# A three-pass matmul kernel of seven layers: another order of products and weight splits at the seams between phases

## Chip, cores, metric

One Trainium2 chip, one core. The metric is device time in microseconds of one execution, from the first instruction to the last with what lies around them. Engines: PE (matmul and transposes), DVE (vector), ACT (scalar), POOL (GpSimd), SP (issues the weight loads).

## What is computed

Sequence 256, width 1024, all in float32. The first block is a short-convolution mixer and a SwiGLU network, then sliding-window attention and a second SwiGLU. The second block is a SwiGLU, a latent-attention and retention layer, a last SwiGLU and a final norm. Each sublayer reads a normalised copy of the running state `h` and adds its branch to it:

```
h = h + rmsnorm(short_conv_mixer(rmsnorm(h, g0)), p0)        # MIX,  8 column blocks
h = h + rmsnorm(swiglu(rmsnorm(h, g1)), p1)                  # FFN1, 11 blocks
h = h + rmsnorm(attention(rmsnorm(h, gkv), rmsnorm(h, gq)), p2)
h = h + rmsnorm(swiglu(rmsnorm(h, g3)), p3)                  # FFN2
h = h + 0.5 * swiglu_2(rms_norm(h, g4))                      # FFN3
h = h + concat(mla(n), retention(n)) @ w_o, n = rms_norm(h, g5)
h = h + 0.5 * swiglu_2(rms_norm(h, g6))                      # FFN4
out = rms_norm(h, final_norm)
```

## The kernel before

The 256 rows are two row tiles, t = 0 and t = 1, of 128 rows. Every float32 product is made in three passes (L1626): high part of x times high part of w, high times low, low times high. So every weight chunk (128 x 1024) is split once: ACT copies it to a rounded high part (`w_high`, L1026), DVE subtracts to get the low part (`w_low`, L1295). Split chunks lie in a ring of 12 slots; chunk c + 12 can be split only when row tile 1 has used chunk c. SP loads raw chunks four ahead into a ring of four (L821 to L828), a load starting when the split of the chunk four before it is done.

Making x for a phase takes this chain for each row tile: `turn` (eight PE transposes of `h` into pG and pT, L1656; DVE multiplies them by the gain into `hg`, L1321; ACT squares `h`, L1052), then `parts` (ACT rounds to `xTh`, L1058; DVE subtracts to `xTl`, L1328; POOL makes the norm factor). The attention needs a second x from the same transposes with another gain: `second` (L1071, L1341), which makes `x2h` and `x2l`.

A phase of blocks (MIX, FFN1 to FFN4) goes block by block: G (the products into pG, 24 matmuls of 512 columns for an FFN, of 384 for MIX), an activation on ACT and DVE (L1114, L1414), T (two transposes, then `aTh` on ACT, L1134, and `aTl` on DVE, L1433; in MIX a convolution with `aTh` and `aTl` made by step Y), D (the product back into pD: 12 matmuls, in MIX 6). At the end of a branch, `tail` squares it on ACT (L1101), POOL makes its norm factor, DVE multiplies by the post gain (L1392), and `join` adds it to `h` on DVE (L1404, two halves). FFN3, the latent layer and FFN4 have no post norm, so their `join` alone follows the product.

One written-out list of steps is walked by every engine (`walk`, L517): each engine issues its own part of each step, in the order of the list, and its queue is strictly in that order. So the place of a step in the list sets both when PE reaches it and what stands in front of it on ACT and DVE. Step R and the helper `refill` (L149) issue splits: ACT's `w_high` and DVE's `w_low` of as many chunks as are named, from the list `freed` of used slots.

The seams are hand-written. `walk_last_follower` (L232) is the end of a phase: G of row tile 1's last block, the `turn` of row tile 0 for the next phase behind it, D of the block before, `parts` of row tile 0, T, and splits. Row tile 1's last product and tail (`end_of`, L536, which calls `last_product`, L249) are left to the next phase: in FFN phases they run behind the first G (`open_end`, L166), followed by T, `refill` of all that is freed, and `join` of row tile 1. Attention and latent phases have no such hook: the last product and join come before them (L545, L550).

The attention's projections are `project(j, t, c)`: column group j (0 reads x, 1 and 2 read x2), row tile t, weight chunk c; four chunks make one group of 24 matmuls (5.5 us). With c == 3 ACT empties the group's bank to `qkv` (L1151). Before a product of row tile t starts, PE waits for that tile's x parts:

```
high, low = (x2h, x2l) if j else (xTh, xTl)
if c % 2 == 0:
    pe.wait_ge(xT_ready[t], xT_base(B_INDEX) + (2 if j else 0) + c // 2 + 1)
```

Then `rope` (L1441, rotary on DVE for the first part), QKT (transposes of q and k; DVE copies `qT`, L1458), S (scores), E, N, PT, PV. In the latent phase `project(i, t, c)` is the like for five groups (group 0 has 416 columns and is emptied to `lat`, L1193), and LAT(t) is three transposes of `lat`. `finish` (L1077 on ACT, L1347 on DVE, L995 on POOL) is the final norm and the stores.

Of the kernel before, what the change touches and what calls it, by code (L numbers as in the profile page):

```python
# [31 lines left out]
ALU = mybir.AluOpType  # L32
# [175 lines left out]
def walk_follower(ph, b, shift, step, freed):  # L208

    if ph.mixer and b == 1:  # L210
        walk_second_follower(ph, shift, step, freed)
        return
    g, first, last = ph.g_chunk(b), b == 0, b == ph.nb - 1
    early = (0 if ph.mixer else 2) if first else 1 if ph.mixer else 3
    step("R", g, early, shift)
    step("G", 1, b, shift)
    if not ph.mixer:
        step("R", g + early, ph.cg - early, shift)
        early = ph.cg
    if not first:  # L220
        step("D", 1, b - 1, shift)
    if ph.mixer:
        step("R", g + early, ph.cg - early, shift)
    if not first:
        step("T", 1, b, shift)
    if not first and not last:
        step("R", ph.d_chunk(b - 1), ph.kd, shift)
    if ph.mixer and not first:
        step("Y", 1, b, shift)


def walk_last_follower(ph, step, freed):  # L232

    b = ph.nb - 1
    g = ph.g_chunk(b)
    early = 0 if ph.mixer else 3
    step("R", g, early, 0)
    step("G", 1, b, 0)
    step("turn", 0, ph.index + 1)
    step("D", 1, b - 1, 0)  # L240
    step("parts", 0, ph.index + 1)
    step("T", 1, b, 0)
    if ph.mixer:
# [12 lines left out]
def walk_phase(eng, ph, step, trips, freed, open_end=None):  # L256

    per = RING // (ph.cg + ph.kd)
    start = 3 if trips else ph.nb
    for s in range(start):  # L260
        walk_block_step(ph, s, 0, step, freed, open_end)
    if trips:
        with eng.Fori(0, trips) as turn:
            for s in range(start, start + per):
                walk_block_step(ph, s, turn, step, freed)
        for s in range(start + per * trips, ph.nb):
            walk_block_step(ph, s, 0, step, freed)
# [10 lines left out]
    step("join", 0, ph.index)  # L278
    walk_last_follower(ph, step, freed)


def walk_attention(step, freed):


    def project(j, t, c):
# [4 lines left out]
    def projects(j, t, cs=range(4)):  # L290
        for c in cs:
            project(j, t, c)
# [4 lines left out]
            freed.append(B_WO + kt)  # L297

    projects(0, 0, range(3))
    walk_prep(step, 1, B_INDEX)  # L300
    project(0, 0, 3)
    step("second", 0)
    refill(step, freed)
    projects(0, 1)
    step("second", 1)
    refill(step, freed, 2)
    projects(1, 0)
    step("rope", 0, 0)
    refill(step, freed)
    step("exp_table",)  # L310
# [78 lines left out]
    output(1, 3)  # L389
    step("join", 0, B_INDEX)  # L390
    output(1, 4)
    refill(step, freed, 4)
    walk_prep(step, 0, B_INDEX + 1)
    for kt in range(5, 7):
        output(1, kt)
    refill(step, freed, 2)


def walk_latent(step, freed):


    def project(i, t, c):
# [13 lines left out]
            freed.append(C_WO + kt)  # L416

    projects(0, 0)
    walk_prep(step, 1, C_INDEX)
    refill(step, freed, 2)  # L420
    projects(1, 0)
    step("LAT", 0)
    refill(step, freed)
    projects(0, 1)
# [92 lines left out]
def walk(eng, step):  # L517
    freed = []
    step("start",)
    step("turn", 0, 0)  # L520
    step("first", 0, 0, FIRST_BEFORE_TURN)
    step("parts", 0, 0)
    step("turn", 1, 0)
    step("first", 0, FIRST_BEFORE_TURN, KT)
    step("fill", 0, 1)
    step("G", 0, 0, 0, ph=MIX)
    step("first", 1, 0, KT // 2)
    step("fill", 1, 1)
# [16 lines left out]
    end_of(FFN1)  # L545
    step("join", 1, FFN1.index)
    walk_attention(lambda *a: step(*a, ph=None), freed)
    walk_phase(eng, FFN2, lambda *a: step(*a, ph=FFN2), 4, freed, end_of_attention)
    walk_phase(eng, FFN3, lambda *a: step(*a, ph=FFN3), 4, freed, lambda: end_of(FFN2))
    end_of(FFN3)  # L550
    step("join", 1, FFN3.index)
    walk_latent(lambda *a: step(*a, ph=None), freed)
    walk_phase(eng, FFN4, lambda *a: step(*a, ph=FFN4), 3, freed)


# [10 lines left out]
def build(nc, x_in, stream, consts_in, table_in, pos_in, posts_in, out):  # L566
    with ExitStack() as ctx:
# [445 lines left out]
        def _(sc):  # L1013
# [61 lines left out]
                return sc.activation(hg[t][:, cols], hg[t][:, cols], ACT.Copy, scale=rr[t])  # L1075

            def finish(ph):  # L1077
                left, right, third, fourth = slice(0, 512), slice(512, 1024), slice(512, 768), slice(768, 1024)
# [6 lines left out]
                sc.wait_ge(h_ready[1], 2 * (LAST - 1) + 3)  # L1085
                sc.activation(junk[1][:, fourth], h[1][:, fourth], ACT.Square, scale=D ** -0.5,
                              accum_out=ss_end).then_inc(ss_ready[1], 1)
# [192 lines left out]
        def _(ve):  # L1280
# [66 lines left out]
            def finish(ph):  # L1347
# [23 lines left out]
                branch_done(ve, 1, k, 1)  # L1371
                ve.wait_ge(h_ready[1], 2 * k + 2)
                added(1, fourth, pT[0][:, 0:256])
                ve.wait_ge(ss_ready[1], 2 * LAST + 2)
                chain(ve.tensor_scalar(ms[1], ss[1][:, 0:1], ss[1][:, 1:2], EPS, ALU.add, ALU.add))
                joined()
                ve.wait_ge(ss_ready[1], 2 * LAST + 3)
                ve.tensor_scalar(ms[1], ms[1], ss_end, None, ALU.add).then_inc(end_m, 1)
                ve.wait_ge(h_ready[1], 2 * k + 3)
# [709 lines left out]
```

## Time and profile before

| what | value |
|---|---|
| median of 3 runs | 1074.96 us (1074.68 to 1077.29) |
| the profiled execution's own time | 1074.11 us |
| its span, first to last instruction | 1072.2 us |
| PE busy | 1055.5 us, 98% |
| PE weight loads | 872.1 us, 81% |
| DVE busy | 655.8 us, 61% |
| ACT busy | 560.9 us, 52% |
| POOL busy | 101.4 us, 9% |
| chain that ended last, PE's share | 89% |
| share of it of DVE's split of low parts | 3% |
| mean granted clock of TensorE | 0.999 |

The execution's own time is 1.9 us above its span, which lies around the span. The phases follow each other in the trace at about 105 us (FFN1's first product), 296 (attention), 376 (FFN2), 562 (FFN3), 753 (latent), 879 (FFN4) and 1060 (finish). A row of the time order gives start, length, engine, line, operation, what is written and read, count, and in brackets the idle time of the engine before it and who ended it; rows with a count above 1 are merged, and their length is from the first start to the last end. A PE row's length is modelled and overlaps the next one.

### The profile page before, as it was taken

To read this page: it belongs to the slowest core of one execution; us is meant where nothing else is said; L and a number is where in the kernel's file an instruction comes from. 1 tells how busy PE (TensorE), PEld (TensorE's weight loads), DVE (VectorE), ACT (ScalarE), POOL (GpSimd) and SP (SyncE) were. 2 spreads that over 40 slices of the span, in tenths; PEclk is the share of its full clock that TensorE was granted. 3 is DMA by queue.
4 is the path that set the end of the run, shared out by engine and by line. 5 is a ranking of instruction groups with operands and counts; after the bars stand their busy time and mean duration, and the time that the engine had idled before them with its cause. 6 is when DMAs were issued, how large, how long until landed. Compare 5 with 4: busy or idle time off the path is not lost.

```text
span 1072.2 us, 14824 instructions
## 1 busy us (share of the span) xinstructions
PE 1055.5 (98%) x5047; PEld 872.1 (81%) x5047; DVE 655.8 (61%) x930; ACT 560.9 (52%) x907; POOL 101.4 (9%) x194
## 2 busy tenths in 40 slices
PE   9999999999999999999999999999999999999997
PEld 6898888888787788888888888887888888888886
DVE  5867654545787864554666455466568674645543
ACT  5756544544667664444555444455476534444542
POOL 0034000000012041000001000000027120000001
PEclk9999999999999999999999999999999999999999
DMA  8664546556561454645565465556545133646541
GB/s 337 197 232 157 181 160 210 181 171 215 196 196 61 136 180 159 223 165 196 192 205 174 157 225 158 202 194 215 159 157 177 61 122 114 202 165 220 162 152 40
DMA packets 51884, 187.81 MB, mean 175 GB/s; under 512 B 5808, under 2 KB 5952, under 8 KB 51840
## 3 DMA queue, kind: packets, MB, share of 16 engines
q1 hardware_dynamic: 50688, 183.79, 51.3%
q0 software_dynamic: 864, 3.07, 0.8%
q8 instruction: 27, 0.44, 0.2%
q10 hardware_dynamic: 288, 0.37, 0.1%
q14 instruction: 17, 0.14, 0.0%
HBM read 186.15 MB, written 1.05 MB: 175 GB/s over the span
## 4 chain that ended last, share of the span: by engine, by line
PE 89%; DVE 6%; ACT 2%; issue 1%; DMA 1%; POOL 0%; POOLq 0%; ACTq 0%; DVEq 0%; SPq 0%
PE pG L1629 16%; PE pG L1631 16%; PE pG L1630 16%; PE pD L1629 11%; PE pD L1631 11%; PE pD L1630 11%; PE pT L1634 3%; DVE w_low L1295 3%; PE pG L1651 1%; PE pG L1634 1%; PE pT L1945 1%; PE pG L1932 1%; ACT w_high L1026 1%; PE pD L1906 1%; PE pT L1772 1%
## 5 line engine op out<-in xcount | busy, mean ns | idle before, releaser
L1295 DVE TENSOR_TENSOR w_low<-raw,w_high 128x1024 fp32r<-128x1024 f32 x340 | 412.5, 1232 | 118.8 <-ACT w_high L1026 105.3
L1026 ACT ACTIVATE w_high<-raw 128x1024 fp32r<-128x1024 f32 x340 | 352.5, 1055 | 79.4 <-PE pG L1631 67.6
L1629 PE MATMUL pG<-w_high,xTh 128*128 128x512 f32 (+1 forms) x816 | 319.9, 392 | 1.7 <-DVE xTl L1328 1.6
L1631 PE MATMUL pG<-w_high,xTl 128*128 128x512 f32 (+1 forms) x816 | 312.4, 383 | 0.0
L1630 PE MATMUL pG<-w_low,xTh 128*128 128x512 f32 (+1 forms) x816 | 312.1, 382 | 0.0
L1631 PEld LDWEIGHTS pG<-w_high,xTl 128*128 128x128 f32 x816 | 153.1, 188 | 28.0
L1629 PEld LDWEIGHTS pG<-w_high,xTh 128*128 128x128 f32 x816 | 153.2, 188 | 27.8 <-DVE xTl L1328 2.6
L1630 PEld LDWEIGHTS pG<-w_low,xTh 128*128 128x128 f32 x816 | 153.5, 188 | 25.6
L1629 PE MATMUL pD<-w_high,aTh 128*128 128x512 f32 x384 | 151.0, 393 | 2.4 <-DVE aTl L1433 2.4
L1631 PE MATMUL pD<-w_high,aTl 128*128 128x512 f32 x384 | 149.9, 390 | 0.0
L1630 PE MATMUL pD<-w_low,aTh 128*128 128x512 f32 x384 | 149.4, 389 | 0.0
L1114 ACT ACTIVATE gate<-pG,stat 128x256 f32<-128x256 f32 x104 | 49.2, 474 | 166.0 <-PE pG L1631 165.5
L1134 ACT ACTIVATE aTh<-pT 128x256 fp32r<-128x256 f32 x88 | 33.7, 383 | 150.5 <-PE pT L1634 150.4
L1433 DVE TENSOR_TENSOR aTl<-pT,aTh 128x256 fp32r<-128x256 f32 x88 | 37.3, 424 | 118.5 <-ACT aTh L1134 118.5
L1414 DVE SCALAR_TENSOR_TENSOR act<-pG,stat,gate 128x256 f32<-128x256 f32 x88 | 42.4, 482 | 98.7 <-ACT gate L1114 98.7
L1629 PEld LDWEIGHTS pD<-w_high,aTh 128*128 128x128 f32 x384 | 72.1, 188 | 16.8 <-DVE aTl L1433 2.8
L1631 PEld LDWEIGHTS pD<-w_high,aTl 128*128 128x128 f32 x384 | 72.0, 188 | 15.1
L1630 PEld LDWEIGHTS pD<-w_low,aTh 128*128 128x128 f32 x384 | 72.2, 188 | 14.0
L1629 PE MATMUL pD<-w_high,xTh 128*128 128x512 f32 (+1 forms) x160 | 64.5, 403 | 0.3 <-DVE xTl L1328 0.3
L1631 PE MATMUL pD<-w_high,xTl 128*128 128x512 f32 (+1 forms) x160 | 62.0, 387 | 0.0
L1630 PE MATMUL pD<-w_low,xTh 128*128 128x512 f32 (+1 forms) x160 | 61.8, 386 | 0.0
L1634 PE MATMUL pT<-consts,act 128*128 128x128 f32 x192 | 37.9, 271 | 0.5 <-DVE act L1414 0.5
(266 smaller groups left out, 827.7 us busy)
## 6 DMA issues: line engine op xcount, KB each, us to landing
raw<-in_stream SPq DMA_DIRECT2D x340, 512.0 KB, 4.3
post<-in_posts POOLq DMA_DIRECT2D x5, 512.0 KB, 4.9
early<-in_stream SPq DMA_DIRECT2D x4, 512.0 KB, 12.5
first_w<-in_stream SPq DMA_DIRECT2D x3, 512.0 KB, 6.0
h<-in_x SPq DMA_DIRECT2D x2, 512.0 KB, 5.6
out<-hg SPq DMA_DIRECT2D x3, 256.0 KB, 2.5
consts<-in_consts POOLq DMA_DIRECT2D x1, 416.0 KB, 4.7
out<-hg ACTq DMA_DIRECT2D x1, 256.0 KB, 2.7
```

The lines of the kernel that those rows point to most:

```text
L1026: sc.activation(w_high[:, slot(static):slot(static) + CHUNK], raw_of(static), ACT.Copy).then_inc(w_high_done, 1)
L1114: sc.activation(gate[t][:], pG[t][:, 0:256], ACT.Copy if ph.mixer else ACT.Silu, scale=rr[t]).then_inc(gate_ready[t], 1)
L1134: sc.activation(aTh[t][:].rearrange("p k r -> p (k r)"), pT[t][:, 0:256], ACT.Copy).then_inc(ah_ready[t], 1)
L1295: ve.tensor_tensor(w_low[:, slot(static):slot(static) + CHUNK], raw_of(static), w_high[:, slot(static):slot(static) + CHUNK].bitcast(F32), ...
L1414: ve.scalar_tensor_tensor(act[t][:], pG[t][:, 256:512], rr[t], gate[t][:], ALU.mult, ALU.mult).then_inc(act_ready[t], 1)
L1433: ve.tensor_tensor(aTl[t][:].rearrange("p k r -> p (k r)"), pT[t][:, 0:256], aTh[t][:].rearrange("p k r -> p (k r)").bitcast(F32), ALU.sub ...
L1629: pe.matmul(dst, ah, hi, start=start, stop=False)
L1630: pe.matmul(dst, ah, lo, start=False, stop=False)
L1631: return pe.matmul(dst, al, hi, start=False, stop=stop)
L1634: return pe.transpose(dst, src, ident)
L1651: mm = pe.matmul(pG[t][:, 0:MIX.cols], hg[t][:, kt * P:(kt + 1) * P], first_w[:, kt * MIX.cols:(kt + 1) * MIX.cols], start=kt == 0, stop=k ...
L1772: mm = pe.matmul(pT[p][:, P * keys * x:P * keys * (x + 1)], qT[t][part, 4 * a + first + x, :], kT[part, a, 0:P * keys], start=True, stop=True)
```

## The change

Four edits of the written order of steps, and one of the final norm.

1. MIX: the splits behind G and T of block 6 (two chunks, and one chunk) are no longer issued there but put on the `freed` list; one chunk is split behind the join of row tile 0, two between `parts` of row tile 0 and T of row tile 1's last block, two behind its Y (before: three there).
2. FFN phases: of the last block's four splits ahead of G of row tile 1, two instead of three come first; three follow behind T, as before, and one is left over for the next phase.
3. Attention and latent: the last product of row tile 1 of the phase before, its tail and join are put in between the first column groups of row tile 0, as in the diff, and the `turn` and `parts` of row tile 1 come behind group 1 of row tile 0. The attention's `second` of row tile 0 comes ahead of the last product.
4. The attention's end: one split ahead of the making of x for FFN2 and four behind two more products, instead of four and two.
5. Final norm: the square of the last 256 columns of row tile 1 is summed by DVE (scale and epsilon in the same instruction) instead of ACT.

```
 def walk_follower(ph, b, shift, step, freed):
...
-    if ph.mixer:
+    if ph.mixer and b == ph.nb - 2:
+        freed += [*range(g + early, g + ph.cg), ph.d_chunk(b - 1)]
+    elif ph.mixer:
         step("R", g + early, ph.cg - early, shift)
     if not first:
         step("T", 1, b, shift)
-    if not first and not last:
+    if not first and not last and not (ph.mixer and b == ph.nb - 2):
         step("R", ph.d_chunk(b - 1), ph.kd, shift)
 def walk_last_follower(ph, step, freed):
...
-    early = 0 if ph.mixer else 3
+    early = 0 if ph.mixer else 2
     step("R", g, early, 0)
     step("G", 1, b, 0)
     step("turn", 0, ph.index + 1)
     step("D", 1, b - 1, 0)
     step("parts", 0, ph.index + 1)
+    freed += [*range(g + early, g + ph.cg), *range(ph.d_chunk(b - 1), ph.d_chunk(b - 1) + ph.kd)]
+    if ph.mixer:
+        refill(step, freed, 2)
     step("T", 1, b, 0)
     if ph.mixer:
         step("Y", 1, b, 0)
-    freed += [*range(g + early, g + ph.cg), *range(ph.d_chunk(b - 1), ph.d_chunk(b - 1) + ph.kd)]
-    refill(step, freed, 3)
+    refill(step, freed, 2 if ph.mixer else 3)
 # walk_phase, behind step("join", 0, ph.index):
+    if ph.mixer:
+        refill(step, freed, 1)
     walk_last_follower(ph, step, freed)
 # walk_attention:
     projects(0, 0, range(3))
+    step("second", 0)
+    refill(step, freed, 2)
+    project(0, 0, 3)
+    open_end()
+    step("join", 1, FFN1.index)
+    projects(1, 0)
     walk_prep(step, 1, B_INDEX)
-    project(0, 0, 3)
-    step("second", 0)
     refill(step, freed)
     projects(0, 1)
     step("second", 1)
     refill(step, freed, 2)
-    projects(1, 0)
     step("rope", 0, 0)
...
     step("join", 0, B_INDEX)
     output(1, 4)
-    refill(step, freed, 4)
+    refill(step, freed, 1)
     walk_prep(step, 0, B_INDEX + 1)
     for kt in range(5, 7):
         output(1, kt)
-    refill(step, freed, 2)
+    refill(step, freed, 4)
 # walk_latent:
     projects(0, 0)
-    walk_prep(step, 1, C_INDEX)
+    open_end()
+    step("join", 1, FFN3.index)
     refill(step, freed, 2)
     projects(1, 0)
+    walk_prep(step, 1, C_INDEX)
     step("LAT", 0)
     refill(step, freed)
     projects(0, 1)
 # finish, on ACT:
-                sc.wait_ge(h_ready[1], 2 * (LAST - 1) + 3)
-                sc.activation(junk[1][:, fourth], h[1][:, fourth], ACT.Square, scale=D ** -0.5,
-                              accum_out=ss_end).then_inc(ss_ready[1], 1)
 # finish, on DVE:
                 added(1, fourth, pT[0][:, 0:256])
+                ve.wait_ge(h_ready[1], 2 * k + 3)
+                chain(ve.tensor_tensor_reduce(junk[1][:, fourth], h[1][:, fourth], h[1][:, fourth], 1.0 / D, EPS, ALU.mult, ALU.add, ss_end))
+                joined()
                 ve.wait_ge(ss_ready[1], 2 * LAST + 2)
-                chain(ve.tensor_scalar(ms[1], ss[1][:, 0:1], ss[1][:, 1:2], EPS, ALU.add, ALU.add))
+                chain(ve.tensor_scalar(ms[1], ss[1][:, 0:1], ss[1][:, 1:2], None, ALU.add))
                 joined()
-                ve.wait_ge(ss_ready[1], 2 * LAST + 3)
                 ve.tensor_scalar(ms[1], ms[1], ss_end, None, ALU.add).then_inc(end_m, 1)
-                ve.wait_ge(h_ready[1], 2 * k + 3)
                 weighted(1, left).then_inc(end_w, 1)
```

## Rows read from the trace of the kernel before

**Rows 1.** The page, part 1: busy time, share of the span, instructions.

```profile
PE 1055.5 (98%) x5047; PEld 872.1 (81%) x5047; DVE 655.8 (61%) x930; ACT 560.9 (52%) x907; POOL 101.4 (9%) x194
```

**Rows 2.** Waits of the tensor engine in the whole span: total, times, longest.

```profile
PE pD L1629 <- DVE aTl L1433: 2.4, 2, 1.4
PE pG L1629 <- DVE xTl L1328: 1.6, 2, 1.3
```

**Rows 3.** Tensor engine in time order, around 300 to 318 us: start, length, what.

```profile
299.74 0.60 PE L1634 MATMUL pG<-consts,h 128*128 128x128 f32 x4
...
300.53 0.48 PE L1629 MATMUL pD<-w_high,xTh 128*128 128x512 f32 x1
...
302.51 0.50 PE L1629 MATMUL pD<-w_high,xTh 128*128 128x512 f32 x1 [0.34 <-DVE xTl L1328]
...
308.07 0.39 PE L1629 MATMUL pD<-w_high,x2h 128*128 128x512 f32 x1
...
317.60 0.81 PE L1634 MATMUL pD<-consts,qkv 128*128 128x128 f32 x6
```

**Rows 4.** Scalar engine in time order, at 308 us.

```profile
308.27 0.69 ACT L1151 ACTIVATE qkv<-pD,stat 128x512 f32<-128x512 f32 x1 [1.45 <-PE pD L1631]
```

**Rows 5.** Vector engine in time order, 285 to 319 us.

```profile
285.66 3.49 DVE L1295 TENSOR_TENSOR w_low<-raw,w_high 128x1024 fp32r<-128x1024 f32 x3
...
309.57 1.29 DVE L1328 TENSOR_TENSOR x2l<-hg,x2h 128x512 fp32r<-128x512 f32 x2
...
314.43 0.77 DVE L1450 TENSOR_TENSOR rtmp<-qkv,consts 128x96 f32<-128x96 f32 x4 [0.95 <-ACT qkv L1151]
...
315.58 2.35 DVE L1295 TENSOR_TENSOR w_low<-raw,w_high 128x1024 fp32r<-128x1024 f32 x2
318.45 0.69 DVE L1458 COPY qT<-pD 128x512 f32<-128x512 f32 x1 [0.52 <-PE pD L1634]
```

**Rows 6.** Tensor, then vector engine, at the start of the latent phase.

```profile
757.58 0.60 PE L1634 MATMUL pG<-consts,h 128*128 128x128 f32 x4
...
759.60 1.29 DVE L1328 TENSOR_TENSOR xTl<-hg,xTh 128x512 fp32r<-128x512 f32 x2
```

**Rows 7.** Tensor, scalar, then vector engine, from mixer to FFN1.

```profile
102.01 0.66 PE L1634 MATMUL pG<-consts,h 128*128 128x128 f32 x4 [1.12 <-DVE h L1404]
...
112.40 0.44 PE L1634 MATMUL pT<-consts,act 128*128 128x128 f32 x2 [0.31 <-DVE act L1414]
...
107.38 2.94 ACT L1026 ACTIVATE w_high<-raw 128x1024 fp32r<-128x1024 f32 x3
...
101.20 1.41 DVE L1404 SCALAR_TENSOR_TENSOR h<-hg,stat,h 128x512 f32<-128x512 f32 x2
...
104.25 1.29 DVE L1328 TENSOR_TENSOR xTl<-hg,xTh 128x512 fp32r<-128x512 f32 x2
106.06 0.74 DVE L1428 SCALAR_TENSOR_TENSOR yT<-cv,consts,yT 128x128 f32<-128x128 f32 x2 [0.52 <-ACT yT L1131]
...
107.50 0.29 DVE L1438 TENSOR_TENSOR aTl<-yT,aTh 128x128 fp32r<-128x128 f32 x1 [0.38 <-ACT aTh L1142]
108.45 3.50 DVE L1295 TENSOR_TENSOR w_low<-raw,w_high 128x1024 fp32r<-128x1024 f32 x3 [0.66 <-ACT w_high L1026]
```

**Rows 8.** Vector engine, from attention to FFN2.

```profile
369.27 4.62 DVE L1295 TENSOR_TENSOR w_low<-raw,w_high 128x1024 fp32r<-128x1024 f32 x4
...
387.30 1.41 DVE L1404 SCALAR_TENSOR_TENSOR h<-hg,stat,h 128x512 f32<-128x512 f32 x2
```

**Rows 9.** Vector engine at the end; then the row of one line, in ns.

```profile
1067.07 0.21 DVE L1378 TENSOR_SCALAR stat<-stat 128x1 f32<-128x1 f32 x1 [0.73 <-ACT junk L1086]
...
L1468 DVE CUSTOM_DVE_ANT_0 sm<-pT,consts x32: 277/354/426, 320.9 to 359.4; 128x128 f32<-128x128 f32 x16, 128x256 f32<-128x256 f32 x16
```

**Rows 10.** Busy us and granted clock of a stretch; then the warm-ups' line, in ns.

```profile
280.00:322.00 42.00, 40.23 (x199) 32.77 (x198) 35.48 (x57) 28.20 (x46) 5.73 (x15) 1.00 0.64 212
...
L1640 PE MATMUL pD<-warm x11: 379/608/634, 1.2 to 4.8; 128*128 128x512 bf16 x11
```

More of the change, by code:

```diff
@@ L221, in walk_follower @@
         step("D", 1, b - 1, shift)
-    if ph.mixer:
+    if ph.mixer and b == ph.nb - 2:
+        freed += [*range(g + early, g + ph.cg), ph.d_chunk(b - 1)]
+    elif ph.mixer:
         step("R", g + early, ph.cg - early, shift)
@@ L225, in walk_follower @@
         step("T", 1, b, shift)
-    if not first and not last:
+    if not first and not last and not (ph.mixer and b == ph.nb - 2):
         step("R", ph.d_chunk(b - 1), ph.kd, shift)
@@ L235, in walk_last_follower @@
     g = ph.g_chunk(b)
-    early = 0 if ph.mixer else 3
+    early = 0 if ph.mixer else 2
     step("R", g, early, 0)
@@ L241, in walk_last_follower @@
     step("parts", 0, ph.index + 1)
+    freed += [*range(g + early, g + ph.cg), *range(ph.d_chunk(b - 1), ph.d_chunk(b - 1) + ph.kd)]
+    if ph.mixer:
+        refill(step, freed, 2)
     step("T", 1, b, 0)
@@ L244, in walk_last_follower @@
         step("Y", 1, b, 0)
-    freed += [*range(g + early, g + ph.cg), *range(ph.d_chunk(b - 1), ph.d_chunk(b - 1) + ph.kd)]
-    refill(step, freed, 3)
+    refill(step, freed, 2 if ph.mixer else 3)
 def last_product(ph, step, freed):
@@ L278, in walk_phase, with walk_attention @@
     step("join", 0, ph.index)
+    if ph.mixer:
+        refill(step, freed, 1)
     walk_last_follower(ph, step, freed)
-def walk_attention(step, freed):
+def walk_attention(step, freed, open_end):
     def project(j, t, c):
@@ L299, in walk_attention @@
     projects(0, 0, range(3))
+    step("second", 0)
+    refill(step, freed, 2)
+    project(0, 0, 3)
+    open_end()
+    step("join", 1, FFN1.index)
+    projects(1, 0)
     walk_prep(step, 1, B_INDEX)
-    project(0, 0, 3)
-    step("second", 0)
     refill(step, freed)
@@ L306, in walk_attention @@
     refill(step, freed, 2)
-    projects(1, 0)
     step("rope", 0, 0)
@@ L391, in walk_attention @@
     output(1, 4)
-    refill(step, freed, 4)
+    refill(step, freed, 1)
     walk_prep(step, 0, B_INDEX + 1)
@@ L395, in walk_attention, with walk_latent @@
         output(1, kt)
-    refill(step, freed, 2)
-def walk_latent(step, freed):
+    refill(step, freed, 4)
+def walk_latent(step, freed, open_end):
     def project(i, t, c):
@@ L418, in walk_latent @@
     projects(0, 0)
-    walk_prep(step, 1, C_INDEX)
+    open_end()
+    step("join", 1, FFN3.index)
     refill(step, freed, 2)
     projects(1, 0)
+    walk_prep(step, 1, C_INDEX)
     step("LAT", 0)
@@ L544, in walk @@
     walk_phase(eng, FFN1, lambda *a: step(*a, ph=FFN1), 4, freed, lambda: end_of(MIX))
-    end_of(FFN1)
-    step("join", 1, FFN1.index)
-    walk_attention(lambda *a: step(*a, ph=None), freed)
+    walk_attention(lambda *a: step(*a, ph=None), freed, lambda: end_of(FFN1))
     walk_phase(eng, FFN2, lambda *a: step(*a, ph=FFN2), 4, freed, end_of_attention)
     walk_phase(eng, FFN3, lambda *a: step(*a, ph=FFN3), 4, freed, lambda: end_of(FFN2))
-    end_of(FFN3)
-    step("join", 1, FFN3.index)
-    walk_latent(lambda *a: step(*a, ph=None), freed)
+    walk_latent(lambda *a: step(*a, ph=None), freed, lambda: end_of(FFN3))
     walk_phase(eng, FFN4, lambda *a: step(*a, ph=FFN4), 3, freed)
@@ L1077, in finish @@
             def finish(ph):
-                left, right, third, fourth = slice(0, 512), slice(512, 1024), slice(512, 768), slice(768, 1024)
+                left, right, third = slice(0, 512), slice(512, 1024), slice(512, 768)
                 square(0, LAST, 0)
@@ L1084, in finish @@
                               accum_out=ss[1][:, 1:2]).then_inc(ss_ready[1], 1)
-                sc.wait_ge(h_ready[1], 2 * (LAST - 1) + 3)
-                sc.activation(junk[1][:, fourth], h[1][:, fourth], ACT.Square, scale=D ** -0.5,
-                              accum_out=ss_end).then_inc(ss_ready[1], 1)
                 sc.wait_ge(end_r, 1)
```

7 lines of the change are left out of this document (4 added, 3 removed).

## The prediction

> **What bounds the kernel now.** I read the page first: PE is busy 98% of the span [rows 1]. No product is added or dropped, so the time can change only by what PE waits for, and all its idle time is under 17 us. The list of waits comes next: behind DVE's `aTl` it waits twice, behind `xTl` twice for a G, 4.0 us together [rows 2]. The time order places them at the seams between phases, where x for the next phase is made while ACT and DVE also split weights. A PE row's length overlaps the next row, so a stall is longer than its bracket; I take start to start. From 302.51 to 308.07 stand 24 matmuls, 0.23 each [rows 3]; PE comes to the x2 product of 302.51 0.5 late. With 0.16 to 0.25 added so, the four waits of rows 2 are 1.7 (attention's seam, `aTl`), 1.2 (latent's), 1.5 (FFN2's, `xTl`) and 0.6 (FFN3's). In MIX's seam PE waits 1.3 for `h` at 102.01 and 0.5 for `act` at 112.40 [rows 7]. What the change can win is thus at most some 7 us, and whatever it uncovers is to be set against that.
>
> **MIX to FFN1.** Three splits are moved from in front of the join of row tile 0. They held up the chain of T, Y, squares, POOL and join by at least one split, 1.14 (four of them take 4.62 [rows 8]), at most by 3.4; I estimate 1.4, and PE's 1.3 for `h` goes. But DVE's next work in the list is now one split between the join and the making of x. Joins end at 101.2 instead of 102.6 [rows 7], split at 102.35, then act, two gain multiplies, the round and the first `xTl`: I get G(0,0) at 104.7 against 105.0 before, so only 0.3 is kept of 1.3. Behind x, two splits now stand ahead of T on both engines. ACT, whose last square lies beside those low parts, is free at 105.1, splits to 107.1, then the convolution: DVE is free of its two low parts at 108.5, and from there to `aTl` it needs what it needs from 106.06 to 107.79, 1.7 [rows 7]: 110.2. That is just when PE ends G(0,0) (5.5 long) and wants D, so no stall there, and no cushion. Two more `w_high` can start on ACT only behind `aTh`, at 109.8, the first lands at 110.8, DVE's two low parts end at 113.2, and behind them is FFN1's first act: T at 113.65 instead of 112.40, +1.25. Before, three splits stood there, but begun at 107.38 on ACT and 108.45 on DVE [rows 7]. One chunk more is left over, so three splits stand ahead of the join of row tile 1 instead of two, and the turn is late another 0.3. Sum +1.55; bounds +0.3 (only the order inside G matters) and +2.2.
>
> **FFN1 to attention.** One split fewer ahead of x: DVE's three took 3.49 from 285.66 [rows 5], x and `aTl` come 1.1 earlier. PE now goes from T straight to group 0 of row tile 0, whose x is ready by then, and its last product comes 5.5 later: the 1.7 goes wholly. The 0.5 at 302.51 goes too, but turns into more, since what covered it is moved away. Four new gaps:
> (a) Behind `turn` of row tile 1, PE's next step is group 0 of row tile 1, which needs that turn's x. Before, one chunk (6 matmuls, 1.36) lay between. The like in the latent phase took from 757.58 to the end of the first `xTl`, half of 1.29 behind 759.60, 2.7 [rows 6]; the turn itself lasts 0.8 [rows 3]; the eviction ahead on ACT is 0.08 longer. So 1.95; bounds 1.6 and 2.3.
> (b) Behind group 0 of row tile 1 came group 1 of row tile 0, which had long been ready; now comes group 1 of row tile 1, which needs `x2l` of row tile 1. ACT's list has the eviction of group 0 ahead of the rounding of x2, so the chain starts only when PE is done: PE's next product started at 308.07, the eviction at 308.27 [rows 4], the first `x2l` ended half of 1.29 behind 309.57 [rows 5]. 2.2 in which PE has nothing; before, it had 24 matmuls. DVE has 5.5 for two splits and two gain multiplies, which is enough. Bounds 1.9 and 2.6.
> (c) Rope comes nearer by that group: behind `x2l` DVE has two splits, 2.35 [rows 5], then rope, 1.15 from 314.43 to the split behind it. That is 12.1 behind the start of group 0, and PE is at the transposes of q and k at 11.85: 0.3; bounds 0 and 0.7.
> (d) Two more splits stand ahead of the copy of `qT`, which took place 0.85 behind the transposes' start at 317.60 with DVE idle before it [rows 3, 5]. Now they end at 14.4, the copy at 15.05, the scores could start at 14.2: 0.85; bounds 0.2 and 1.3.
> Nothing else is late: `second` of row tile 0 ends at 299, when its group starts; the join at 303.8, a us ahead of the turn. Sum −1.7 −0.5 +1.95 +2.2 +0.3 +0.85 = +3.1.
>
> **Attention to FFN2.** Three splits fewer ahead of x, 3.4 of DVE's time (four took 4.62 [rows 8]): the 1.5 goes. But one more chunk is left over, so three splits instead of two stand ahead of the join of row tile 1. That join starts at 387.30 [rows 8], and its halves end just as PE takes them; 1.14 later they leave PE 0.5 and 0.2 short. Sum −0.8; bounds −1.3 and −0.3.
>
> **FFN2 to FFN3.** The 0.6 goes by the split that is moved back; the same leftover costs 0.7 at the join. Sum +0.1; bounds −0.3 and +0.3.
>
> **FFN3 to latent.** The 1.2 for `aTl` and 0.1 at the turn go. The turn of row tile 1 has now only LAT(0), three transposes, 0.25, between it and the products that need its x: 1.95 less 0.25 is 1.7. Sum +0.4; bounds −0.1 and +0.8.
>
> **Final norm.** ACT's square and the crossing go. The row nearest in kind, a product summed over 256 columns from PSUM, took 0.43 and its read-out 0.1 [rows 9], here behind `h` at 1066.05. Two small operations of 0.2 follow, so the last ends near 1067.03 where it ended at 1067.28 [rows 9]. Sum −0.2; bounds −0.5 and +0.2.
>
> What this rests on is the price of a split behind a split. DVE's rows give 1.14 from start to start at 1.23 in length [rows 8]. The Trainium skill (VectorE: DVE Perf Modes, The DRAIN you can't avoid) says the next operation starts only when the pipe is empty, after a drain of about the length less 266 ns. By that rule each extra split would cost some 2.2 and the sum would be near +8; the trace doesn't agree with it here.
>
> **Sum.** +1.55 +3.1 −0.8 +0.1 +0.4 −0.2 = +4.15, say 4.2 us. On the profiled execution's 1074.11 that is 1078.3; that one lay 0.85 below the median of 1074.96, and a median is what is compared, so 1079.2. About 0.3%, 3.2 us, is what a measurement of this kernel can tell from no change.
>
> **Rivals.**
> The queues are looser than I draw them. MIX's seam costs no more than 0.3, gaps (c) and (d) shrink, and later waits of the attention take back some: the two long gaps of attention and the one of latent, 5.85, stay against 3.5 that goes there. For it speaks that DVE was only two thirds busy there; against it, that every queue is strictly in order. +0.5 to +3.1, 1075.5 to 1078.1. Chance 0.26.
> Not slower: gaps (a) and (b) don't arise, PE having other work there. That is so only if an x part of row tile 1 is there before its turn is over, which the list excludes as I read it; then 4.15 comes off and the sum is 0.0, with (c) and (d) gone too −1.2: 1073.8. It decides the sign when (a) and (b) together fall below 0. Chance 0.05.
> The clock. Three gaps of about 2 lie within 10 us. In this trace the granted clock stays at 1.00, 2.4 GHz, over stalls of 1.7 [rows 10]; the warm-ups at the start show the other level, 0.61 long against 0.38. If it fell at one of them, a stretch like the start's, eleven in 4.0 where at 0.23 each they take 2.7, would cost 1.3: 1080.5, twice that for two. Chance 0.05. The Trainium skill (TensorE: Matmul & The Clock Gate, Part 1: The HAM clock gate) says that the throttled state is the default and activity lifts it; the rows don't show such gaps as close as these.
> Worse queues: ACT waits for loads (they start four splits back, so late splits load late), another 1 to 3 at MIX and at the joins: 1080.5 to 1082. Chance 0.06.
>
> **How the numbers follow.** My forecast, +3.2 to +5.2, has 0.58. With the rivals: slower 0.58 + 0.05 + 0.06 = 0.69; within 0.3% 0.26 + most of 0.05, with a little for measurement, 0.28; faster 0.03. The range takes the forecast, the looser queues but their lowest end, the clock's and half of the last: 1076.0 to 1081.7.
>
> **What would show it.** In the changed trace: no wait for `aTl` ahead of a last product; PE's list headed by `xTl` in attention and latent (near 2.0 and 1.7) and by `x2l` (2.2), a wait for `qT` near 0.8; at MIX's seam no wait for `h` but one of 2 for `act`; three splits ahead of each join of row tile 1 and PE 0.7 late there. Wrong would make me: PE busy without gap behind the turns of row tile 1, or a T at MIX's seam as early as before.

## The result, and the profile after

The changed kernel takes 1079.03 us (median of 6 runs, 1078.49 to 1079.21), the kernel before 1075.09 beside it (6 runs): a ratio of 1.0033 [1.002, 1.0046]. Slower by 0.33%: the interval lies above 1, though it reaches below the 0.3% that can be told from no change. A second set of runs of the same kernel gave 1.0042 [1.0028, 1.0057] (after_again, below). The forecast was 1079.2.

| what | before | after |
|---|---|---|
| profiled execution's own time | 1074.11 us | 1078.84 us |
| its span | 1072.2 us | 1077.0 us |
| PE busy | 1055.5 us | 1057.3 us |
| mean granted clock | 0.999 | 0.996 |

The page of the changed kernel, part 1 and the chain that ended last by engine, against [rows 1]:

```profile
PE 1057.3 (98%) x5047; PEld 873.2 (81%) x5047; DVE 657.0 (61%) x932; ACT 560.6 (52%) x905; POOL 104.4 (10%) x194
...
PE 92%; DVE 4%; ACT 2%; issue 1%; POOL 0%; POOLq 0%; ACTq 0%; DVEq 0%
```

The matmuls are as many as before. The waits of PE have other names. Of the changed kernel, total, times, longest, against [rows 2]:

```profile
PE pD L1634 <- DVE xTl L1332: 3.2, 2, 1.8
PE pD L1634 <- DVE x2l L1332: 2.0, 1, 2.0
PE pT L1639 <- DVE act L1419: 2.0, 2, 1.8
PE pG L1634 <- DVE xTl L1332: 1.2, 1, 1.2
PE pD L1645 <- DVE warm L1308: 1.2, 1, 1.2
PE pG L1639 <- DVE h L1409: 1.0, 2, 0.5
```

The 2.4 for `aTl` of [rows 2] is gone; 3.2 for `xTl` ahead of pD and 2.0 for `x2l` are new, and so are `act` (MIX) and `h` (the joins). PE in time order, changed kernel, one row for each such place, then the first scores:

```profile
104.40 0.50 PE L1634 MATMUL pG<-w_high,xTh 128*128 128x512 f32 x1 [1.19 <-DVE xTl L1332]
113.28 0.44 PE L1639 MATMUL pT<-consts,act 128*128 128x128 f32 x2 [1.75 <-DVE act L1419]
...
309.07 0.50 PE L1634 MATMUL pD<-w_high,xTh 128*128 128x512 f32 x1 [1.75 <-DVE xTl L1332]
...
316.84 0.50 PE L1634 MATMUL pD<-w_high,x2h 128*128 128x512 f32 x1 [2.02 <-DVE x2l L1332]
...
324.80 0.38 PE L1777 MATMUL pT<-kT,qT 64*128 64x128 f32 x2
...
392.67 0.66 PE L1639 MATMUL pG<-consts,h 128*128 128x128 f32 x4 [0.48 <-DVE h L1409]
...
769.39 0.46 PE L1634 MATMUL pD<-w_high,xTh 128*128 128x416 f32 x1 [1.43 <-DVE xTl L1332]
```

The row at 392.67 is the turn of row tile 1 in FFN2. DVE's rows in front of it show the chunk left over, three splits where there were two, and the join behind them:

```profile
388.46 3.50 DVE L1299 TENSOR_TENSOR w_low<-raw,w_high 128x1024 fp32r<-128x1024 f32 x3 [0.20 <-ACT w_high L1033]
391.88 1.41 DVE L1409 SCALAR_TENSOR_TENSOR h<-hg,stat,h 128x512 f32<-128x512 f32 x2
```

Start to start, less the usual pitch, PE loses 2.00 at 309.07 (gap a), 2.18 at 316.84 (gap b) and 1.68 at 769.39. Why gap (b): ACT, then DVE, of the changed kernel:

```profile
314.85 0.69 ACT L1155 ACTIVATE qkv<-pD,stat 128x512 f32<-128x512 f32 x1 [3.47 <-PE pD L1636]
315.44 1.14 ACT L1065 ACTIVATE x2h<-hg 128x512 fp32r<-128x512 f32 x2
```

```profile
316.09 1.29 DVE L1332 TENSOR_TENSOR x2l<-hg,x2h 128x512 fp32r<-128x512 f32 x2 [2.06 <-ACT x2h L1065]
```

ACT had been idle for 3.47 when the eviction started. The rounding of x2 stands behind it in the list, so it waits until PE has finished the group, and PE then waits for it.

One thing was not in the forecast's main case. In this execution the granted clock fell behind gap (b). Busy times of a stretch (the third number from the end is the granted clock), and a PE row in it, of the changed kernel:

```profile
317.00:322.00 5.00, 5.00 (x16) 3.92 (x17) 4.79 (x10) 4.65 (x5) 0.00 (x0) 0.66 0.42 120
```

```profile
318.58 0.63 PE L1634 MATMUL pD<-w_high,x2h 128*128 128x512 f32 x1
```

The same two of after_again:

```profile
317.00:322.00 5.00, 5.00 (x25) 4.03 (x26) 4.79 (x10) 4.97 (x6) 0.00 (x0) 1.00 0.33 115
```

```profile
318.38 0.39 PE L1634 MATMUL pD<-w_high,x2h 128*128 128x512 f32 x1
```

In the first, products stand 0.43 apart from 318.16 to 321.14 (1.2 GHz) and 0.23 again from 321.52 (2.4 GHz). So after_again, with no fall, is the profile in which the steps can be read. By seam, in us between two events that every kernel has (MIX: first mixer D to the first product behind the turn of row tile 1 in FFN1; front: turn of row tile 0 to the first scores; the next two: turn of row tile 0 to behind that of row tile 1; latent: turn of row tile 0 to the latent scores):

| kernel | MIX | front | att. to FFN2 | FFN2 to 3 | latent | median |
|---|---|---|---|---|---|---|
| before | 96.44 | 32.36 | 18.52 | 19.14 | 57.84 | 1075.1 |
| after | 98.09 | 36.00 | 17.86 | 19.48 | 58.29 | 1079.0 |
| after_again | 98.12 | 35.26 | 17.86 | 19.48 | 58.27 | 1078.8 |
| att_back | 98.17 | 31.89 | 17.86 | 19.48 | 58.29 | 1075.3 |
| cover | 98.13 | 35.32 | 17.85 | 19.48 | 58.26 | 1079.1 |
| mix_back | 96.59 | 35.97 | 17.86 | 19.48 | 58.26 | 1078.1 |
| no_leftover | 98.56 | 35.50 | 18.93 | 18.55 | 58.27 | 1080.5 |
| att_spread | 98.19 | 34.83 | 17.85 | 19.48 | 58.24 | 1079.0 |
| lat_spread | 98.12 | 35.27 | 17.86 | 19.47 | 56.74 | 1077.6 |
| all_seams | 95.91 | 34.92 | 18.93 | 18.55 | 56.74 | 1075.5 |
| join_two | 97.48 | 35.27 | 16.93 | 18.54 | 58.28 | 1076.5 |
| att_four | 98.35 | 30.73 | 17.86 | 19.47 | 58.27 | 1074.8 |
| tuned | 95.13 | 30.71 | 16.93 | 18.55 | 56.73 | 1068.8 |

The stretches between the seams stay within 0.1 of before in all of them, but for FFN2 and FFN3 in no_leftover and all_seams (0.36 longer each). MIX's column holds most of the MIX phase too, and differs by up to 0.47 between kernels with one and the same MIX. The kernel before had medians of 1074.73 to 1075.09 beside these runs.

At the end, DVE sums the last 256 columns, against [rows 9] (changed kernel, DVE):

```profile
1071.20 0.42 DVE L1379 CUSTOM_DVE_ANT_0 junk<-h 128x256 bf16<-128x256 f32 x1
1071.55 0.08 DVE L1379 DVE_READ_ACCUMULATOR2_ANT stat<- 128x1 f32 x1
1071.66 0.21 DVE L1382 TENSOR_SCALAR stat<-stat 128x1 f32<-128x1 f32 x1
```

From PE's last matmul (1070.10; 1064.99 before) to the end of the span it is 6.9 where it was 7.2. All kernels below have this edit and the same end (6.94 to 6.96); none was run without this edit alone.

### The profile page after: what moved, and what is told of

Same layout as the page of the kernel before. It is cut to its first block, busy times and chain, and to the rows that moved or that the text cites. A ratio compares the mean times of both kernels' runs of the same rounds, so it can differ in the third digit from the quotient of the medians.

```text
span 1077.0 us, 14824 instructions
## 1 busy us (share of the span) xinstructions
PE 1057.3 (98%) x5047; PEld 873.2 (81%) x5047; DVE 657.0 (61%) x932; ACT 560.6 (52%) x905; POOL 104.4 (10%) x194
## 4 chain that ended last, share of the span: by engine, by line
PE 92%; DVE 4%; ACT 2%; issue 1%; POOL 0%; POOLq 0%; ACTq 0%; DVEq 0%
PE pG L1636 16%; PE pG L1635 16%; PE pG L1634 16%; PE pD L1634 12%; PE pD L1636 11%; PE pD L1635 11%; PE pT L1639 3%; DVE w_low L1299 2%; PE pG L1656 1%; PE pG L1639 1%; PE pT L1950 1%; PE pG L1937 1%; ACT w_high L1033 1%; PE pD L1911 1%; PE pT L1777 1%
```

## The experiments

**after_again**: the changed kernel, unchanged.

> The changed kernel once more, for a second profile. In the first one TensorE's granted clock fell behind the second long gap of the attention's first stage (0.66 over 317 to 322 us) and PE had no wait for rope or for qT. Theory Q (each queue strictly in order): the gaps for xTl and x2l of row tile 1, 2.0 and 2.2 us, come in every execution. Where the clock stays at 1.00 behind them, the waits for rope and qT forecast at 0.3 and 0.85 stand in the place of the slow stretch, and the scores start at the same time within 0.5 us; the time is 1079.0 either way. Theory C (the clock decides): without the fall the execution is 1.5 us shorter, about 1077.5, and with it 1079.

1078.81 (1078.22 to 1079.82), ratio 1.0042 [1.0028, 1.0057]. Same waits, no clock fall, and now the waits that the slow stretch had covered can be seen; PE, around the scores:

```profile
321.16 0.87 PE L1639 MATMUL pD<-consts,qkv 128*128 128x128 f32 x6
...
324.12 0.60 PE L1777 MATMUL pT<-kT,qT 64*128 64x128 f32 x6 [0.71 <-DVE qT L1463]
```

Transposes of q and k come 0.1 late by rope, the scores 0.87 by `qT`. Theory Q's 1079.0 came; theory C's 1077.5 without the fall did not (the profiled execution took 1078.22). Theory Q's "within 0.5 us" was missed: from the turn to the scores the two profiles differ by 0.74.

**att_back**: the attention's front in the old order, all else as changed.

```
-    projects(0, 0, range(3))
-    step("second", 0)
-    refill(step, freed, 2)
-    project(0, 0, 3)
     open_end()
     step("join", 1, FFN1.index)
-    projects(1, 0)
+    projects(0, 0, range(3))
     walk_prep(step, 1, B_INDEX)
+    project(0, 0, 3)
+    step("second", 0)
     refill(step, freed)
     projects(0, 1)
     step("second", 1)
     refill(step, freed, 2)
+    projects(1, 0)
```

> The changed kernel with the attention's first stage in its old order (last product and join of row tile 1 first, group 1 of row tile 0 between the two groups of row tile 1); all else as changed. Theory Q: the gaps of 2.0 and 2.2 and what follows go, the wait for xTl of 0.5 comes back; the wait for aTl ahead of the last product comes back but shorter, as x is made one split earlier: 0.6 to 1.2 instead of 1.7. Lag of the scores against the kernel before falls from 5.1 to between 0.8 and 1.5 us, time 1074.7 to 1075.6. Rival (the stage loses wherever the last product stands, because one split is left over and DVE is full): the time stays above 1077.

1075.34 (1074.55 to 1076.91), ratio 1.0005 [0.9996, 1.0015]: 3.5 of the loss is in this edit. PE, `aTl` and then `xTl`:

```profile
293.67 0.38 PE L1638 MATMUL pT<-consts,act 128*128 128x128 f32 x2
294.98 0.50 PE L1633 MATMUL pD<-w_high,aTh 128*128 128x512 f32 x1 [0.93 <-DVE aTl L1437]
...
304.70 0.50 PE L1633 MATMUL pD<-w_high,xTh 128*128 128x512 f32 x1 [0.34 <-DVE xTl L1331]
```

The front is 31.89, 0.47 less than before: the split fewer ahead of x gives 0.5 of the 1.7 at `aTl` (1.18 is left). What is left is not a split's: PE comes to T at 293.67 without a wait, and from there the way over ACT and DVE to `aTl` lies bare, as no product stands between T and the last product. Only another order of products can cover it.

**cover**: nine extra matmuls of 512 columns into pG, never read, in gap (b).

```
     projects(0, 1)
+    step("cover", 9)
     step("second", 1)
```

> The changed kernel with nine products more, 512 columns each, from x2 of row tile 0 into the unused bank pG, behind group 0 of row tile 1, where PE waits 2.2 us for x2l; their result is not used. The nine take 2.04 at 0.227. Theory Q: the gap is filled and nothing is later by it, x2l comes when ACT and DVE have made it; the clock stays at 1.00, and instead of the slow stretch PE waits for rope (0.3) and qT (0.8). Time 1078.6 to 1079.1, the scores at most 0.5 earlier. Theory C: without the slow stretch 1.5 us are won, 1077.5. If fillers delay what follows: 1079.5 or more.

1079.1 (1078.09 to 1079.44); front 35.32 against 35.26. Work that fills gap (b) is free: PE had nothing else there. None of its 5 executions shows a mean clock under 0.998, but that is no proof that the filler kept the clock up: no_leftover, below, leaves both gaps open and shows none in 4.

**mix_back**: MIX's splits in the old places.

```
-    if ph.mixer and b == ph.nb - 2:
-        freed += [*range(g + early, g + ph.cg), ph.d_chunk(b - 1)]
-    elif ph.mixer:
+    if ph.mixer:
...
-    if ph.mixer:
-        refill(step, freed, 2)
...
-    refill(step, freed, 2 if ph.mixer else 3)
+    refill(step, freed, 3)
...
-    if ph.mixer:
-        refill(step, freed, 1)
```

> The changed kernel with MIX's splits in their old places (three behind block 6 and three behind Y of the last follower, none behind the join). Theory Q: PE waits 1.3 for h again and 0.3 for xTl, but T of FFN1's first block is back at 0.5 instead of 1.9, and only two splits stand ahead of the join: the lag of 1.65 at this seam goes, time 1077.3 to 1077.7. Rival (the first turn is what counts at this seam, as the moved splits were meant to show): time rises by 1.3, to above 1080.

1078.06 (1076.96 to 1078.87), ratio 1.0031 [1.0019, 1.0043]: its seam falls by 1.5 as theory Q has it, the median by 0.8 to 1.0 only, which leaves it 0.4 above the 1077.3 to 1077.7 expected. The rival's 1080 did not come. The seam is the surer reading: the start, which no edit here touches, differs by up to 1.5 between profiles, and this median is of 7 executions. PE:

```profile
103.12 0.66 PE L1633 MATMUL pG<-consts,h 128*128 128x128 f32 x4 [1.12 <-DVE h L1403]
...
113.51 0.44 PE L1633 MATMUL pT<-consts,act 128*128 128x128 f32 x2 [0.30 <-DVE act L1413]
```

The wait for `h` is back and the 1.75 for `act` gone.

**no_leftover**: the chunk left over at each end of phase is split there.

```
-    refill(step, freed, 2 if ph.mixer else 3)
+    refill(step, freed, 2 if ph.mixer else 4)
...
-    refill(step, freed, 4)
+    refill(step, freed, 5)
```

> The changed kernel with four splits instead of three behind the last T of each FFN phase, and five instead of four at the attention's end, so that no chunk is left over and two splits, as before the change, stand ahead of the join of row tile 1 in FFN2 and in FFN3. Strict queues: the waits for h at these two joins (0.65 and 0.25 in each, start to start) go, the rest stays: 1.8 less than the changed kernel, 1077.2 where that has 1079.0. Rival, that the split is paid wherever it stands (DVE late again ahead of the turn of row tile 1): 1079.0, with waits of the same sum for xTl or xTh behind the turn.

1080.47 (1079.44 to 1080.79), ratio 1.005 [1.0034, 1.0065]: 1.5 worse, where 1.8 better was expected. FFN2 to FFN3 gains the 0.93, but the attention's end loses 1.07, and FFN2 and FFN3 take 0.36 more each (in steps of some 0.03 a block inside G; why stays open): +0.86. The front takes 0.2 more, and MIX, not touched, shows 0.45 more in this profile, at an `act` in the middle of the phase. ACT, then PE, at the attention's end:

```profile
380.03 3.89 ACT L1033 ACTIVATE w_high<-raw 128x1024 fp32r<-128x1024 f32 x4
385.88 1.06 ACT L1033 ACTIVATE w_high<-raw 128x1024 fp32r<-128x1024 f32 x1 [1.96 <-DMA raw<-in_stream]
386.96 1.28 ACT L1118 ACT_TABLE_LOAD   x1
388.26 0.47 ACT L1118 ACTIVATE gate<-pG,stat 128x256 f32<-128x256 f32 x1
```

```profile
389.31 0.44 PE L1639 MATMUL pT<-consts,act 128*128 128x128 f32 x2 [1.80 <-DVE act L1419]
```

The fifth split of a burst waits for its load, and a table load of 1.28 and the activation of the next block stand behind it in ACT's queue. In the changed kernel the table load follows the four splits and ACT then idles 0.96 before the activation; the 1.06 of a ready fifth `w_high` would about fit into that (an estimate), the 1.96 for the load does not. From start to start this T comes 1.95 later than in the changed kernel, and the join behind it gets 0.9 back. My theory counted only DVE's time.

**lat_spread**: in the latent phase, three ready chunks behind the last product, and a whole ready group behind the turn of row tile 1.

```
-    projects(0, 0)
+    project(0, 0, 0)
     open_end()
+    projects(0, 0, range(1, 4))
     step("join", 1, FFN3.index)
+    walk_prep(step, 1, C_INDEX)
     refill(step, freed, 2)
     projects(1, 0)
-    walk_prep(step, 1, C_INDEX)
```

> The changed kernel with three chunks of the latent phase's group 0 of row tile 0 behind the last product of row tile 1, and the turn of row tile 1 ahead of two splits and of group 0 of row tile 1's products with a ready group between. Strict queues: the wait of 1.68 for xTl behind the turn becomes at most 0.1: 1.6 less than the changed kernel, 1077.4. Rival, that DVE is late with the join by the splits left over: a wait for h of 0.5 to 1 ahead of the turn, 1078.0 to 1078.5.

1077.57 (1076.84 to 1078.52), ratio 1.0025 [1.0015, 1.0036]; latent seam 56.74 against 58.27, 1.53 less. As expected.

**att_spread**: the same idea in the attention; none of FFN1's four is split at its end, so the first `refill` below splits six. `project(1, 0, 0)` is the first chunk of group 1 of row tile 0, which is ready; the expectation below calls it one of group 0 of row tile 1. All of group 0 of row tile 1 (`projects(0, 1)`) follows it, then the other three chunks of the ready group. The front is now:

```
+    project(0, 0, 0)
+    step("second", 0)
+    open_end()
+    project(0, 0, 1)
+    project(0, 0, 2)
+    step("join", 1, FFN1.index)
+    walk_prep(step, 1, B_INDEX)
+    project(0, 0, 3)
+    project(1, 0, 0)
+    refill(step, freed)
+    projects(0, 1)
+    step("second", 1)
+    projects(1, 0, range(1, 4))
+    refill(step, freed, 2)
```

> The changed kernel with another front of the attention: the last product of row tile 1 behind one chunk of group 0 of row tile 0, the join behind two more, the turn of row tile 1 ahead of the fourth, then the first chunk of group 0 of row tile 1 only, and group 1 of row tile 0 between it and the other three. Every making of x then has at least one chunk or group that is ready. Strict queues: the two gaps of 2.0 and 2.2 behind the turn and ahead of the first product with x2 of row tile 1 go, and most of the 0.9 for qT: the stage from the turn in FFN1 to the scores of row tile 0, 203.7 to 204.4 in the changed kernel, becomes 199 to 199.6; 1074.0 to 1074.6 in all. Looser or other limits (DVE saturated in that stretch): a wait for h at the join or for aTl of 0.5 to 2, and 1075 to 1077. No gain at all, 1079.0, if the gaps were not what the change cost.

1079.0 (1078.31 to 1080.52), where 1074.0 to 1074.6 was expected; the stage is 203.2 instead of 199 to 199.6. The time is the one named for "the gaps were not what the change cost", but the trace shows otherwise: both gaps went, one of 2.7 for `x2l` came, and behind it the clock fell (0.66 from 315 to 320). ACT's rows name it:

```profile
303.97 3.89 ACT L1035 ACTIVATE w_high<-raw 128x1024 fp32r<-128x1024 f32 x4
309.55 1.06 ACT L1035 ACTIVATE w_high<-raw 128x1024 fp32r<-128x1024 f32 x1 [1.68 <-DMA raw<-in_stream]
311.94 1.06 ACT L1035 ACTIVATE w_high<-raw 128x1024 fp32r<-128x1024 f32 x1 [1.34 <-DMA raw<-in_stream]
312.91 0.67 ACT L1157 ACTIVATE qkv<-pD,stat 128x512 f32<-128x512 f32 x1
314.89 1.23 ACT L1067 ACTIVATE x2h<-hg 128x512 fp32r<-128x512 f32 x2 [1.31 <-DVE hg L1327]
```

Four raw chunks are there; the fifth and sixth wait. DVE's low part of the sixth and then `hg` stand behind them, and the rounding of x2 waits 1.31 for `hg`.

**all_seams**: att_spread, lat_spread, no chunk left over in FFN2 and FFN3, and in MIX one put-off split instead of three. MIX's part of the edit:

```
     if ph.mixer and b == ph.nb - 2:
-        freed += [*range(g + early, g + ph.cg), ph.d_chunk(b - 1)]
+        step("R", g + early, 1, shift)
...
+    if ph.mixer and b == ph.nb - 2:
+        step("R", g + 2, 1, shift)
+        freed.append(ph.d_chunk(b - 1))
```

> All of it together: the fronts of att_spread and lat_spread, no chunk left over ahead of the joins in FFN2 and FFN3, and in MIX only one of the three splits put off (behind Y of the last block), the other two back at G and behind T of block 6. Strict queues, seam by seam against the kernel before: MIX 0 to -0.7, attention's front -1.3 to -1.7, attention to FFN2 -1.5, FFN2 to FFN3 -0.6, latent -1.2, final norm -0.2: 4.8 to 5.9 less, 1068.9 to 1070.0 by a median of 1074.8. If gains at one seam are lost at the next (the chunks have to be split somewhere): 1071 to 1074. If the seams do not add up at all: 1074.8 or more.

1075.46 (1074.5 to 1076.69), ratio 1.0007 [0.9998, 1.0016]. This misses the 1068.9 to 1070.0, and the 1071 to 1074 too. MIX −0.53 against before, FFN2 to FFN3 −0.59 and latent −1.10 are as expected; the front (+2.56) and the attention's end (+0.41) are those of att_spread and no_leftover, with their waits for loads, and FFN2 and FFN3 have no_leftover's 0.36 each.

**join_two**: at most two splits ahead of a join of row tile 1; the third behind the next T.

```
         step("T", 0, 0, shift)
-        refill(step, freed)
+        refill(step, freed, 2)
         step("join", 1, ph.index - 1)
```

> The changed kernel with at most two splits ahead of the join of row tile 1 in every FFN phase; the one left over follows behind the next T of row tile 0. no_leftover split it ahead of the first T instead, and paid 1.95 there for act, behind a w_high that waited 1.96 for its weight load. Theory, that a split costs only what it holds up: the waits for h ahead of the turn of row tile 1 go in FFN1 (0.31 and 0.25), FFN2 and FFN3 (0.65 and 0.25 each), nothing comes in their place: 2.4 less than the changed kernel, 1076.5. Rival, that each phase pays for the chunk wherever it stands: 1079.0, with new waits for act or aTl in the block behind.

1076.54 (1075.4 to 1077.62), ratio 1.0015 [1.0005, 1.0024]. −0.64, −0.93 and −0.94 at three seams, nothing later: 2.5 in all. The chunk that made the T at the attention's end 1.95 late in no_leftover costs nothing here.

**att_four**: att_spread's products, with bursts of at most four.

```
     step("second", 0)
+    refill(step, freed, 1)
     open_end()
...
-    refill(step, freed)
+    refill(step, freed, 4)
     projects(0, 1)
     step("second", 1)
+    refill(step, freed, 1)
     projects(1, 0, range(1, 4))
-    refill(step, freed, 2)
     step("rope", 0, 0)
-    refill(step, freed)
+    refill(step, freed, 3)
...
     step("S", 0)
+    refill(step, freed, 1)
```

> att_spread with the same products in the same order, but no burst of six splits in front of the making of x2 of row tile 1: one ahead of the last product of row tile 1, four behind the turn, one behind x2, three and one later. In att_spread the fifth and the sixth w_high waited 1.7 and 1.3 for their weight loads, and x2 came 2.7 late behind them. Theory, that loads were what held it up: the 2.7 goes, no wait of ACT for raw in front of x2, the stage from the turn in FFN1 to the scores of row tile 0 becomes 199.5 (203.2 in att_spread, 200.8 before the change); about 1075.2. Rival, that DVE and not the loads set it: the gap shrinks by the two splits moved, 2.3, but returns ahead of rope or qT, stage 201.5 or more, 1077 or more.

1074.84 (1073.66 to 1075.22), ratio 0.9996 [0.9987, 1.0005]. The stage of the expectation is 199.13 (168.40 of FFN1 and 30.73 of the front). ACT:

```profile
305.02 3.89 ACT L1037 ACTIVATE w_high<-raw 128x1024 fp32r<-128x1024 f32 x4
...
311.37 1.23 ACT L1069 ACTIVATE x2h<-hg 128x512 fp32r<-128x512 f32 x2
312.50 1.05 ACT L1037 ACTIVATE w_high<-raw 128x1024 fp32r<-128x1024 f32 x1
```

No wait for raw, and x2 starts as soon as PE's group is emptied. Against att_spread the front fell by 4.1: the gap of 2.7 is gone, and with it the stretch at the lower clock that followed it. The rival's 201.5 did not come. How much of the 2.7 was load and how much the two splits' own time on DVE (2.3) was not separated; the chain in ACT's rows of att_spread, where both `w_high` start at their load's end, speaks for the load.

**tuned**: att_four's front, lat_spread's, join_two's limit, all_seams' MIX.

> att_four's front, lat_spread's, join_two's limit, and MIX as in all_seams, in one kernel. Seam by seam against the kernel before, if each part keeps what it does alone: MIX -0.5, attention's front -1.3, attention to FFN2 -1.5, FFN2 to FFN3 -0.5, latent -1.1, final norm -0.2: 5.1 less, 1069.7 by a median of 1074.8. If the loads or DVE take back att_four's part: 1071 to 1072. If the parts don't add up: 1074 or more.

1068.81 (1067.84 to 1069.27), ratio 0.9944 [0.993, 0.9957]: 6.2 faster than before, 10.2 than the changed kernel, and 0.9 below the 1069.7 expected. Its waits of PE, from the longest:

```profile
PE pD L1649 <- DVE warm L1312: 1.2, 1, 1.2
PE pT L1643 <- DVE act L1420: 0.7, 2, 0.5
PE pT L1781 <- DVE qT L1467: 0.7, 1, 0.7
PE pT L1643 <- DVE act L1423: 0.5, 2, 0.3
```

No x and no `h` is waited for by name. By the table the seams give −1.31, −1.65, −1.59, −0.59 and −1.11: 6.25. All but MIX's are what the single kernels gave; MIX has all_seams' −0.53 and join_two's −0.64, 1.17 together. In all_seams the wait for `h` ahead of the first turn is gone and only the join of row tile 1 costs 0.5; with join_two's limit that goes too. So at MIX's seam one put-off split was enough, and the two others are what cost.

## Why the prediction was right

The working held seam by seam, and the sign and size with it. By the seams of after_again and the end, the change costs 1.68 + 2.90 − 0.66 + 0.34 + 0.43 − 0.28 = 4.4 us, where 4.15 was forecast. That the spans (1076.4 against 1072.2) differ by 4.2 and the medians by 3.9 and 4.1, closer still, is in part luck: the start, 0.2 earlier in the changed kernel's profiles, was no step of mine, and executions of one kernel differ by more than that.

- **MIX to FFN1**: +1.55 forecast, +1.65 and +1.68 measured; 1.76 if counted from the matmul in front of the first turn, as the kernel before also lost 0.15 at an `act` near 54 us. The wait for `h` goes, 1.1 more than before comes at G for `xTl`, so 0.2 of the 1.3 is kept (0.3 forecast); T is then 1.25 late as forecast; the turn of row tile 1 costs 0.5 where I put 0.3. The leftover split at the join was priced too low here as at the two joins below.
- **FFN1 to attention**: +3.1 forecast, 2.90 in after_again. Gap (a) 1.95 and 2.00, (b) 2.2 and 2.18, (c) 0.3 and 0.1, (d) 0.85 and 0.87; the 1.7 and 0.5 went. One step was wrong without touching the sum: I had x and `aTl` come 1.1 earlier by the split fewer. Counted from the turn, att_back's `xTl` comes 1.0 earlier, but its `aTl` only 0.5, since PE is not at T sooner; the new order covers that wait all the same. (The product at 302.51 that I called one of x2 reads x.)
- **Attention to FFN2**: −0.8 and −0.66. **FFN2 to FFN3**: +0.1 and +0.34; at each join I put 0.7, it is 0.65 and 0.25, 0.9, and that is nearly the whole miss; +0.34 lies just outside my bound of +0.3.
- **FFN3 to latent**: +0.4 and +0.45, with 1.7 forecast at the new gap and 1.68 measured.
- **Final norm**: −0.2 and −0.3.

What rested on the price of a split behind a split held. In the changed kernel, as before, four take 4.63, 1.14 from start to start:

```profile
380.08 4.63 DVE L1299 TENSOR_TENSOR w_low<-raw,w_high 128x1024 fp32r<-128x1024 f32 x4 [0.87 <-ACT w_high L1033]
```

The Trainium skill (VectorE: DVE Perf Modes, The DRAIN you can't avoid) gives a drain of about the length less 266 ns behind an operation, but the same paragraph says that a next operation which is not held starts earlier. The prediction left that out; these rows agree with it. The sum near +8 that it drew from the drain alone stands there without its working; it would be a ratio of 1.0074, which both intervals exclude.

**The rivals.** The looser queues fell: gap (d) came in full, and the later stretches took nothing back. The idle DVE that I named for it was a misreading of [rows 10]: DVE was busy 35.48 of 42.00 there, 84%; two thirds is ACT's share. That PE has other work in gaps (a) and (b) fell too. Worse queues by loads did not show at the changed kernel's seams (ACT waits there for a raw chunk once, 0.9 in the latent's, and that seam is 58.29 against 58.27 in after_again), but that mechanism governed no_leftover and att_spread. The clock was the part sized wrongly in both ways. I gave it 0.05; it fell in the profiled execution, and a mean clock of 0.996 marks 5 of 11 executions of the changed kernel. I priced it at 1.3; it stretched 316.84 to the transposes of q and k from 4.27 to 5.83, 1.56, but rope and `qT` were late anyway and 0.83 came back behind them, so the front is 0.74 longer (36.00 against 35.26). In the whole time of the changed kernel it does not stand out: the 5 have a median of 1078.84, the 6 others 1079.06. In join_two, which has the same front, it may: the 3 executions at 0.997 have a median of 1077.48, the 7 others 1076.34. So the 0.74 is read from one pair of profiles and its price in the whole time stays open. That the mean clock marks the fall in executions without a trace is inferred from those with one.

## What to carry to other kernels

When a last product is moved to cover one making of x, look at what covered the next: each making needs its own ready product. Here one wait of 1.7 and one of 0.5 went, and moving the ready groups away brought 5.1 of new ones (2.00, 2.18, 0.1, 0.87). Put a turn in front of work that reads the other tile, and let no burst of splits be longer than the chunks already loaded. A step that is left over is cheap only where nothing in its queue is about to be waited for: at the attention's end one and the same split made the next T 1.95 late in one place and cost nothing one step later.

## What was not expected of the hardware

- **Clock.** The granted clock fell from 1.00 to a stretch of 0.66 behind gaps of 2.0 and 2.2 with 5.5 of products between them, in some executions of the same kernel and not in others; in att_spread it fell behind one gap of 2.7. By the mean clock (0.997 or less), it fell in 5 of 11 executions of the changed kernel, in 2 of 7 of mix_back, 4 of 8 of lat_spread, 3 of 10 of join_two and 0 of 4 of no_leftover, all with gaps (a) and (b), and in 4 of 4 of att_spread. With gap (b) filled it fell in none of 5, nor in tuned's 5, which is too few to say that filling the gap prevents it. In the kernel before, stalls of up to 1.7 left it at 1.00 [rows 10].
- **Loads.** Behind four splits in a row, the fifth chunk's load was issued at 306.45 in att_spread (SP's queue) and its `w_high` began at 309.55, 3.1 later; the sixth began 2.4 behind that, at its own load's end, close to the 2.7 in which PE uses up a chunk (12 matmuls of 0.227). The two loads behind these landed 2.1 and 1.3 apart, so at what pace a longer backlog would be made up stays open.

```profile
306.45 5.92 SPq L834 DMA_DIRECT2D raw<-in_stream  x5
```

- **Start.** The first product of MIX's D begins at 22.0 to 23.5 us in these profiles, with nothing changed ahead of it: spans that differ by under 1.5 say nothing until the start is taken off.
